# Inverting the 16x16 diagonal blocks of the delta rule on GpSimd, one block per partition, and starting TensorE's doubling at size 16

## The reference

```
A[t,s]  = -beta[t] * (k_t . k_s) * exp(g_t - g_s)      for s < t, else 0
inverse = (I - A)^-1                                   128x128, unit triangular
v_new   = inverse * (beta*(V - decayed K S))           S = state after the chunk before
out     = (Q K^T masked, decayed) v_new + decayed Q S
```

## Time and profile before

| | us |
|---|---|
| time of three runs, median | 2266.92 (2266.36 to 2272.52) |
| profiled execution, its own time | 2268.75 |
| its span, first to last instruction | 2266.9 |
| TensorE busy | 2209.0 (97%) |
| VectorE busy | 1570.4 (69%) |
| ScalarE busy | 1394.3 (62%) |
| GpSimd busy | 21.7 (1%) |
| mean granted TensorE clock | 0.988 |

### The profile page before, as it was taken

The page is one execution under the profiler, slowest core; times in us unless marked ns, Lnnn a source line. Parts: engine busy times, 40 slices in busy tenths (PEclk is TensorE's granted clock), DMA queues, the critical chain, the costliest instruction groups (busy, mean ns, idle before and its releaser), DMA issues.

```text
span 2266.9 us, 38597 instructions
## 1 busy us (share of the span) xinstructions
PE 2209.0 (97%) x16098; PEld 2068.5 (91%) x16098; DVE 1570.4 (69%) x2245; ACT 1394.3 (62%) x1918; POOL 21.7 (1%) x14
## 2 busy tenths in 40 slices
PE   8999999999999999999899999999989999998999
PEld 7999999999999999999788888889879999888999
DVE  5777656666467775565689999986867664775664
ACT  6775546544467845364677777776765444765553
POOL 0000000000000000000000000000000000000000
PEclk9999999999999999998899999999999999999999
DMA  7441335556545422332799999964315654423553
GB/s 259 153 146 56 103 94 159 173 172 183 185 149 172 150 75 85 103 132 88 254 342 333 336 334 333 345 239 154 131 47 170 185 186 154 158 75 112 188 184 130
DMA packets 112213, 398.12 MB, mean 176 GB/s; under 512 B 12576, under 2 KB 12704, under 8 KB 112032
## 3 DMA queue, kind: packets, MB, share of 16 engines
q1 hardware_dynamic: 112032, 395.58, 52.5%
HBM read 394.48 MB, written 1.05 MB: 174 GB/s over the span
## 4 chain that ended last, share of the span: by engine, by line
PE 94%; DVE 3%; ACT 2%; issue 1%; DMA 0%; DVEq 0%; SPq 0%; ACTq 0%
PE ps L432 92%; DVE wlo L2040 1%; ACT whi L1280 1%; DVE arena L2040 1%; ACT rst L1290 0%; ACT arena L1290 0%; PE ps L966 0%; ACT arena_r L1290 0%; ACT scr L1290 0%; DVE h L2040 0%; PE ps L883 0%; ACT uh L1290 0%; DMA h<-xT 0%; DVE ul L2048 0%; PE ps L726 0%
## 5 line engine op out<-in xcount | busy, mean ns | idle before, releaser
L2040 DVE TENSOR_TENSOR wlo<-raw,whi 128x1024 fp32r<-128x1024 f32 (+2 forms) x622 | 747.2, 1211 | 381.6 <-ACT whi L1280 376.0
L1280 ACT ACTIVATE whi<-raw 128x1024 fp32r<-128x1024 f32 (+2 forms) x622 | 645.9, 1043 | 424.8 <-PE ps L432 423.7
L432 PE MATMUL ps<-uh,whi 128*128 128x256 f32 x2240 | 649.3, 290 | 3.3 <-issue 1.4
L432 PE MATMUL ps<-ul,whi 128*128 128x256 f32 x2240 | 633.3, 283 | 0.0
L432 PE MATMUL ps<-uh,wlo 128*128 128x256 f32 x2240 | 633.3, 283 | 0.0
L432 PE MATMUL ps<-arena_r,whi 128*128 128x256 f32 x2720 | 490.1, 283 | 7.1 <-DVE arena_r L2040 6.2
L432 PEld LDWEIGHTS ps<-uh,whi 128*128 128x128 f32 x2240 | 427.6, 191 | 14.0 <-issue 9.8
L432 PEld LDWEIGHTS ps<-ul,whi 128*128 128x128 f32 x2240 | 427.6, 191 | 6.7 <-issue 6.2
L432 PEld LDWEIGHTS ps<-arena_r,whi 128*128 128x128 f32 x2720 | 420.1, 189 | 11.3 <-issue 7.7
L432 PEld LDWEIGHTS ps<-uh,wlo 128*128 128x128 f32 x2240 | 427.4, 191 | 0.0
L432 PE MATMUL ps<-arena_r,wlo 128*128 128x256 f32 x1360 | 381.9, 281 | 0.0
(11 more groups left out here) (168 smaller groups left out, 2249.9 us busy)
## 6 DMA issues: line engine op xcount, KB each, us to landing
raw<-stream SPq DMA_DIRECT2D x586, 512.0 KB, 3.8
arena<-stream SPq DMA_DIRECT2D x64, 512.0 KB, 5.6
CO<-stream SPq DMA_DIRECT2D x44, 512.0 KB, 5.6
raw<-stream SPq DMA_DIRECT2D x32, 384.0 KB, 4.6
arena<-stream SPq DMA_DIRECT2D x20, 384.0 KB, 4.3
CO<-stream SPq DMA_DIRECT2D x12, 384.0 KB, 4.6
CO<-const SPq DMA_DIRECT2D x2, 704.5 KB, 7.0
h<-xT SPq DMA_DIRECT2D x4, 256.0 KB, 5.7
```

The source lines that it names most:

```text
L432: return self.e.matmul(o, l, r, start=start, stop=stop, skip_group_check=True)
L1280: self.e.activation(M.whi[:, b:b + n], M.raw[a][:, 0:n], ACT.Copy).then_inc(K.sem("weight_hi"), 1)
L2040: return self.e.tensor_tensor(o, a, b, op)
```

## The change

Levels 0 to 3 leave TensorE, ScalarE and VectorE. Both chunks first make their AT, QKD (now two buffers of each). SyncE then takes the 16x16 diagonal blocks of AT, 64 from a chunk, to DRAM (eight DMAs a chunk, 64 bytes an element) and reads them back as one block per partition, 128 partitions. GpSimd inverts them by elimination, 15 steps of a product and a sum on at most 64 elements a partition, each waiting for the one before, and copies the inverses and their transposes to rows in which they lie on the diagonal of a 32x32 block (`wide`). Two DMAs each take them to DRAM, four DMAs each put them onto the diagonals of X and XT, which GpSimd has cleared. TensorE starts with level 4. `LATER` says how many pieces of weights SyncE issues before each step. The block matrices are in DRAM at other addresses for each layer. The rest of the strings is rearranged.

```diff
+LATER = (3, 6, 6, 10, 10, 11, 12, 4, 5)
...
-            for lev in range(1, 7):
+        for c in range(2):
+            tk = slice(c * P, c * P + P)
+            AT = M.at[c]
+            for lev in range(4, 7):
                 for g in range(2):
                     b = self.bank(work, "y", l, c, lev, g)
...
+                    if lev == 4:
+                        self.wait_ge(K.sem(f"inv{c}"), 64 * (l + 1))
...
                 for g in range(2):
+                    if lev == 4:
+                        self.wait_ge(K.sem(f"invT{c}"), 64 * (l + 1))
...
@@ GpSimd, delta @@
+        self.wait_ge(*K.when("gb", l, 6))
+        self.e.memset(A["S"][:, 256:1024], 0.0).then_inc(*s())
+        self.wait_ge(*s.last)
+        self.e.memset(A["S"][:, 256:512:17], 1.0).then_inc(*s("unit", l))
+        self.e.memset(M.wide[1], 0.0).then_inc(*s())
+        self.e.memset(A["X"], 0.0).then_inc(*s("cleared", l, 0))
+        self.e.memset(A["XT"], 0.0).then_inc(*s("clearedT", l, 0))
         for c in range(2):
             for g in range(2):
                 self.wait_ge(*K.when("qkd", l, c, g))
-            self.e.tensor_tensor(QKD, QKD, wide(M.co("causal")[:, 0:P], P, 8), MUL).then_inc(*s("qkd1", l, c))
+            self.e.tensor_tensor(M.qkd[c], M.qkd[c], wide(M.co("causal")[:, 0:P], P, 8), MUL).then_inc(*s("qkd1", l, c))
+        self.wait_ge(*K.when("unit", l))
+        self.wait_ge(K.sem("blocks"), 16 * (l + 1))
+        for j in range(15):
+            n, w = 15 - j, j + 1
+            x = M.part[j % 2][:, 0:n * w].rearrange("p (n w) -> p n w", w=w)
+            if j:
+                self.wait_ge(*s.last)
+            self.e.tensor_tensor(x, block[:, j, j + 1:16].unsqueeze(2).broadcast_to([P, n, w]),
+                                 inv[:, j, 0:w].unsqueeze(1).broadcast_to([P, n, w]), MUL).then_inc(*s())
+            self.wait_ge(*s.last)
+            self.e.tensor_tensor(inv[:, j + 1:16, 0:w], inv[:, j + 1:16, 0:w], x, ADD).then_inc(*s())
+        self.wait_ge(*s.last)
+        for n, x in enumerate((inv, inv.rearrange("p r w -> p w r"))):
+            for b in range(2):
+                r = slice(64 * b, 64 * b + 64)
+                last = self.e.tensor_copy(v3(M.wide[n], 32)[r, :, 16 * b:16 * b + 16], x[r])
+            last.then_inc(*s(("inv", "invT")[n], l))
+        self.wait_ge(*K.when("ps", "y", l, 0, 6, 1))
+        self.e.memset(A["X"], 0.0).then_inc(*s("cleared", l, 1))
+        self.wait_ge(*K.when("ps", "vn", l, 0, 1))
+        self.e.memset(A["XT"], 0.0).then_inc(*s("clearedT", l, 1))
@@ SyncE @@
+        for c in range(2):
+            after(LATER[c], "decayed", l, c)
+            for g in range(2):
+                self.wait_ge(*K.when("at", l, c, g))
+            for b in range(8):
+                self.e.dma_start(M.eighth(l, c, b), M.diagonal(M.at[c], 16, b)).then_inc(K.sem("decays"), 16)
+        after(LATER[2], "decayed", l, 1)
+        self.wait_ge(K.sem("decays"), 256 * (l + 1))
+        self.e.dma_start(M.block, M.store(l, 0)[0:32768].rearrange("(p j i) -> p j i", p=P, i=16)).then_inc(K.sem("blocks"), 16)
+        for n, key in enumerate(("inv", "invT")):
+            after(LATER[3 + n], "decayed", l, 1)
+            self.wait_ge(*K.when(key, l))
+            rows = M.store(l, 1 + n).rearrange("(n b w) -> b n w", b=2, w=512)
+            for b in range(2):
+                self.e.dma_start(rows[b], M.wide[n][64 * b:64 * b + 64, :]).then_inc(K.sem(f"stored{n}"), 16)
+        for c in range(2):
+            for n, key in enumerate(("X", "XT")):
+                if c:
+                    after(LATER[7 + n], "solved", l, 0)
+                else:
+                    after(LATER[5 + n], "decayed", l, 1)
+                self.wait_ge(K.sem(f"stored{n}"), 32 * (l + 1))
+                self.wait_ge(*K.when(("cleared", "clearedT")[n], l, c))
+                for q in range(4):
+                    self.e.dma_start(M.diagonal(v3(M.A[key], P), 32, q), M.quarter(l, 1 + n, c, q)).then_inc(
+                        K.sem(("inv", "invT")[n] + str(c)), 16)
```

More of the change, by code:

```diff
@@ L267, in sb @@
             return ctx.enter_context(nc.sbuf_tensor(name, [P, n], dt))[:, :]
-        self.stream, self.small, self.const, self.xT, self.pT, self.out = drams
+        self.stream, self.small, self.const, self.xT, self.pT, self.blocks, self.out = drams
         self.SM, self.CO = sb("SM", small_layout()[1]), sb("CO", const_layout()[1])
@@ L298, in __init__ @@
         A = self.A
+        self.at = [v3(A[x], P) for x in ("AT", "VN")]
+        self.qkd = [v3(A[x], P) for x in ("QKD", "D")]
+        self.kd, self.vn = [v3(A[x], P) for x in ("S", "X")], v3(A["AT"], P)
+        self.block, self.inv = (v3(A["S"][:, i * 256:(i + 1) * 256], 16) for i in range(2))
+        self.wide = [A[x][:, 512:1024] for x in ("S", "Y")]
+        self.part = [A["Y"][:, i * 64:(i + 1) * 64] for i in range(2)]
         self.ret = (v3(A["gz_r"]), v3(A["rg_r"]))
@@ L660, in delta @@
         r_b = A["rows"][0:8, 0:T]
-        D, AT, QKD, X, XT, Y = (v3(A[n], P) for n in ("D", "AT", "QKD", "X", "XT", "Y"))
-        S, VN = v3(A["S"], P), v3(A["VN"], P)
+        X, XT, Y, S, VN = (*(v3(A[n], P) for n in ("X", "XT", "Y", "S")), M.vn)
         for c in range(2):
@@ L702, in delta @@
                 for g in range(2):
+                    if lev == 4:
+                        self.wait_ge(K.sem(f"invT{c}"), 64 * (l + 1))
+                    else:
+                        self.wait_ge(*K.when("xt", l, c, lev - 1, g))
                     if lev < 6:
@@ L719, in delta @@
                     yield
-            R, KD = Y, X
+            R, KD, QKD = Y, M.kd[c], M.qkd[c]
             for g in range(2):
@@ L748, in delta @@
                 last.then_inc(*s("ps", "vn", l, c, g))
+                K.marks["solved", l, c] = len(K.pieces)
                 yield
@@ L2272, in delta @@
                     *s(("at", l, c, g), ("free", "bb", l, c, g)))
-                self.wait_ge(*K.when("xi", l, c))
-                self.wait_ge(*s.last)
-                self.e.copy_predicated(XT[:, four, :], M.level(0), a4).then_inc(*s("xt", l, c, 0, g))
                 yield
@@ L2955, in delta @@
         A, s = M.A, self.mark("pool_delta")
-        X, QKD = v3(A["X"], P), v3(A["QKD"], P)
+        X, inv, block = v3(A["X"], P), M.inv, M.block
+        self.wait_ge(*K.when("gb", l, 6))
[5 more added lines that the diff above has]
+        self.e.memset(A["XT"], 0.0).then_inc(*s("clearedT", l, 0))
         for c in range(2):
```

62 lines of the change are left out of this document (35 added, 27 removed).

## The result

| | before | after |
|---|---|---|
| median of the runs beside each other | 2268.74 us (2266.36 to 2272.52, 4 runs) | 2215.18 us (2213.68 to 2220.33, 4 runs) |
| profiled execution, its own time | 2268.75 | 2220.33 |
| its span | 2266.9 | 2218.5 |
| TensorE records | 16098 | 15490 |

The ratio is 0.977, with a 95% interval of 0.9755 to 0.9785: 53.6 us less. The forecast was 2216.

A forecast was written before the change was run, and what follows sets the result against it. TensorE, busy for all of both delta-rule windows, was taken as the bound: 2268.75 - 68 for removed products + 17 for waits and clock = 2217.7, less 1.8 for the runs' median, 2216 us; range 2198 to 2251.

The forecast's parts named there:

- The price: TensorE, both layers: 288 products at 0.224 us and 32 transposes at 0.11 leave, 68 us in all.
- The first `kk` at 146.2: TensorE, first layer: first `kk` product starts at 146.2 instead of 154.87, standing 72 weight products of 0.12 us earlier.
- Level 4 due at 192: TensorE, first layer: after `kk`, `bb`, `qk`, weight pieces and 18 retention products, it would reach level 4 at 192.
- X landed at 198.2: First layer: AT, mask, GpSimd inversion from 176.7 to 190.2, copies, stores and loads make X ready at 198.2.
- wrong if the DMAs take over 3 us each: Sign against the forecast: the DMAs on the inversion's path were counted as landing about 2 us after issue.
- GpSimd's first step right behind its mask: Sign on GpSimd's queue: inversion starts behind the second chunk's QKD mask, at 176.7, 6 us after the blocks have landed.
- even: Level 4: XT is needed three groups later than X and comes some 3 us after it, so no extra wait.
- Level 4 six us late, 8.5 a layer with the clock: TensorE at level 4: 6 us waiting for X plus 2.5 for slow clock, 17 us for both layers.
- the change gives less elsewhere: Rival: `kk` finds key norms not ready or a ring bank held, 3 to 6 us a layer more, 2225 to 2232; chance 0.10.
- fully hidden, 2199: Rival at level 4: GpSimd's chain takes 6 us, X lands at 190.7 before it is due, 2199; chance 0.27.
- The blocking decides: Rival: each GpSimd step waits for a VectorE operation, 30 us in all, 26 a layer lost, 2251; chance 0.18.
- Slower: Rival: small GpSimd operations cost more; slower than before once lateness and clock exceed 34 us a layer, 1.3 us a step; chance 0.05.

The follow-up runs named there:

- unchanged kernel run beside the experiments: The changed kernel itself, run once more without edits on the same chip as its variants: 2216.52 us, ratio 0.9772.
- runs with a shorter chain: Changed kernel with 13 of the 15 elimination steps on GpSimd left out, run twice: 2216.92 us (0.9783) and 2214.75 us (0.977).
- lengthened chain: Changed kernel with every product of the elimination made three times, 60 GpSimd operations in place of 30: 2245.1 us (0.9904).
- moved with its queues: Changed kernel, one branch weight piece ahead of level 4, its DMA before the wait for the inverse, its splits moved earlier: 2218.62 us (0.9798).
- mask behind: Changed kernel with the mask of the second chunk's QKD put behind the inversion in GpSimd's queue: 2219.59 us (0.9783).
- piece ahead: Changed kernel with one branch weight piece put ahead of level 4 in TensorE's order only: 2226.89 us (0.9823).

## Why the prediction was right, and where only its sum was

*"Every product taken from TensorE shortens the kernel by what it costs, as long as the products that are left are not made to wait."* The price was right. In the profiled execution busy time is 63.6 us less and not 68, at a mean granted clock of 0.986 against 0.988 before; in the unchanged kernel run beside the experiments, at 0.988 as before, it is 2209.0 - 2140.9 = 68.1. The condition failed at more places than I named. With the products gone and nothing else changed, half of their time came back as waits and slower clock.

*The first `kk` at 146.2*: 148.88. Two waits of 0.95 and 0.34 for splits, in strings rearranged around 115 and 139 us, and 0.74 for the normalised keys make 2.0 of the 2.7. I had expected no wait for `wlo`.

*Level 4 due at 192*: TensorE reached it at 202.35 - 1.89 = 200.5. That is 2.7 for `kk`, 3.4 for the two waits in between, and some 2 for the work itself. Of these 1.3 are the price of the 48 products `kk`, `bb` and `qk`, where I had 0.224 each: the first 28 of them take 155.89 - 148.88 = 7.0 us, 0.25 each, the four `bb` between the first two starts below 0.27. The rest is spread over pieces and retention.

```profile
149.94 1.15 PE L457 MATMUL ps<-arena,CO 8*128 8x128 f32 x8
151.02 2.05 PE L457 MATMUL ps<-arena 128*128 128x128 f32 x16
...
155.89 0.36 PE L457 MATMUL ps<-uh,whi 128*128 128x256 f32 x1
```

*X landed at 198.2*: 202.35. Step by step: the mask started at 176.45 where I had 173.5, because the products started later; it took 2.42, not 3.2; the chain 14.5, not 13.5; the two copies for `inv` 0.9, as forecast (SyncE's first store is issued at 194.19), and from there to the landing 8.2, not 7.0, because X landed 3.6 us after its last issue, not 2. By the sign "wrong if the DMAs take over 3 us each" that was a miss: the loads of X and XT here took 3.5 from issue to landing, in the median of the whole program 2.7. VectorE's part was right to a microsecond (13.1 from the first four groups of products, done at 153.0, to the last AT for 12.8, 10.2 from there to QKD for 10.9), and so were "GpSimd's first step right behind its mask" and 0.45 us a step (0.48). That XT would come no later than it is wanted ("even") held in the execution above, but not in that of the unchanged kernel beside the experiments, where TensorE waits for it too in the second layer:

```profile
815.04 1.73 PE L457 MATMUL ps<-arena 128*128 128x128 f32 x8 [1.83 <-DMA arena<-blocks]
```

*Level 4 six us late, 8.5 a layer with the clock*: 1.89 late, and 9.3 a layer. This is the step that was wrong in kind. The due time moved by 8.5 and the ready time by 4.1; the rest TensorE loses before level 4, at the convolution's bank and in the retention. I had put this, "the change gives less elsewhere", at 0.10 and as something on top; it is most of the loss, and by the runs with a shorter chain most of it would be there with an inversion for nothing. The forecast of 2216 came true by luck, because two errors cancel: the wait at level 4 was put 4.1 us a layer too long, and five others of 5.5 in all weren't forecast (with the clock 0.8 too dear: 8.5 - 4.1 + 5.5 - 0.8 = 9.1). The rival "fully hidden, 2199" fails for the same reason: taking away the elimination left 2215 to 2217.

*The blocking decides* failed by its count: four of 30 steps were held by a split, 1.1 us each, and a fifth by a shorter product. By the Trainium skill (SBUF — State Buffer, "Who interferes with whom") the one that comes second is blocked for the whole instruction of the other; the trace agrees, the first slow step ending at 180.02 with the first split gone by 179.8 (a third of 3.73 from 178.53). *Slower*: the slope of the lengthened chain, 12.2 us of wait for 11.9 of chain, bears out its reckoning; the kernel was 53.6 / 2 = 27 us a layer away from it.

*What stays open*: whether a new order of all three strings together could end both chains earlier. Only single moves were tried, one or two at a time. Open too is what sets how many stretches at half clock an execution has: the clock's part of every difference above is read and not explained.

## To carry to other kernels

Work taken from an engine that is always busy was also the cover of every chain that ran beside it: read, for each of them, when it will end and when it will be wanted, and not only for the chain that the change adds. Where two paths end together, shortening either one shows little; lengthen one to find its slope, and remove the work without the replacement to find the other. A piece of work is independent only if its DMA, its preparation on the other engines and its place in each queue are; moved alone it cost 10 us, moved with its queues 2 to 6. Read waits and clock apart before a difference of a few us is given a cause.

## What the runs showed of the hardware

- A small dependent GpSimd operation (15 to 64 elements on 128 partitions, waiting for the one before) takes 0.22 to 0.37 us and follows its forerunner at 0.3 to 0.45 where no split lies beside it; added ones cost 0.41 each, those beside splits included. A copy of 64x256 takes 0.4 to 0.6.
- Beside a split, GpSimd's small step takes 0.97 to 1.34 us and VectorE loses nearly nothing (1.24 for 1.22); before, beside a long GpSimd product, it was the split that lost. Beside the convolution, whose products have one operand in PSUM (184.36 to 186.79, 2.43 us, as before), the steps keep their 0.3 us.
- Loads of 32x8x32 (32 KB in runs of 128 bytes) took 3.5 us from issue to landing in the first delta rule (2.7 in the median of all 32), the stores of 8 KB 1.5, those of 128 KB 2.3 and the 128 KB load of the blocks 2.1.
- The same program had its 3.4 us stretches at half clock at different places in two executions (202.8 us in one, 187.4 in the other of the kernel after). Runs of the kernel after lie up to 6.7 us apart, those of its variants up to 15 (mask behind, piece ahead), so differences of a few us between medians of four or five are not told from nothing here.
